# Norms, index scores and key choice of the first block moved in between its input projections; modulation blocks paired anew, the last one formed on VectorE

## The chip, the cores and the metric

One core of a Trainium2 chip runs the whole program. The metric is device time in microseconds (us), the median of three executions. Engines: TensorE (PE, its weight loads PEld), VectorE (DVE), ScalarE (ACT), GpSimd (POOL), and SyncE (SP), whose queue issues the weight loads.

## What is computed

Two transformer-like blocks on 256 tokens of width 1024, float32. The change lies in the first:

```python
ada = c @ w_ada + b_ada                      # 6 x 1024: shift1, scale1, gate1, shift2, scale2, gate2
h = rms_norm(x, g_norm1) * (1 + scale1) + shift1
z = h @ w_in                                 # 3524 wide: q 512, k 64, v 64, iq 256, ik 64, iw 4, p 512, gates 2048
q, k, ik = rms_norm(zq heads), rms_norm(zk), rms_norm(zik)
# index scores: for each query, sum over 4 heads of relu(iq . ik) * iw; the best 64 keys are attended
y_attn = dsa_attention(q, k, zv, iq, ik, iw) @ w_up_attn
y_pool = pool_mixer(zp, w_pool_grp, s_pool) @ w_up_pool    # means over windows 2, 4, 8, 16, then mixed per group
g_attn, g_pool = sigmoid(zg)
x = x + gate1 * ((g_attn * y_attn + g_pool * y_pool) @ w_out)
h2 = rms_norm(x, g_norm2) * (1 + scale2) + shift2
x = x + gate2 * peer_ffn(h2, ...)            # product-key experts: scores of 8 heads, top 16 of 16384 rows of u and v
```

The second block (recurrent branch, sparse attention, convolved feed-forward) isn't touched.

## The kernel before

All weights come through one stream of blocks, each 4 quarters of 512 KB. `plan()` writes out their order; two blocks that `PAIRED` joins are interleaved quarter by quarter (`quarter_no`). SP loads quarter b into `ring[b % 4]` once the quarter before it in that slot has left (L438), strictly in order. The blocks of `SPLIT` (in, pq, u, v and later ones) are split into a rounded part `high` (ScalarE, `round_quarter`, L925) and a rest `low` (POOL, L1918), four slots each, chosen by b % 4 too. `high` of a slot is written again only when TensorE has multiplied the quarter before in it; the ring slot is free when POOL is done. Split products are three matmuls (L340 to L342). up_pool, up_attn and out blocks are multiplied straight from the ring in float32 (L338; two matmul records for each product). `ahead(name, q)` on ScalarE rounds every split quarter up to three places beyond the named one, in ScalarE's own order of work.

The modulation (`ada0` to `ada11`, 512 columns each) is formed on VectorE as a running sum over the ring's quarters (L1453, L1455: 8 instructions a block) and then summed over the partitions by TensorE with a vector of ones (L475, or L470 and L471 for the two gate1 blocks 4 and 5). ada8 alone was multiplied on TensorE: 64 products of one column (L486).

Order in the first block: ada0 to ada3; the norm n1; in0 to in6 (`token_major`, 48 matmuls each), whose results ScalarE copies to Z (L1033). After the last one: VectorE's squares of q, k and ik (L1496, L1497), their norms into N1 (L1498 to L1517) and ScalarE's root; TensorE's pool means (L626) and pool mixing (L632) with ScalarE's copies (L1039, L1043) between; up_pool in three pieces, and between them the turning of N1 (L461) and the index products (L647). ScalarE applies relu to these (L1051), VectorE weights them into scores (L1527, L1529) and chooses keys by eight rounds of MAX8 and MATCH_REPLACE8 for each half of the tokens (L1540, L1541; the mask by L1543). ScalarE makes the sigmoids of the gates (L1054) and copies y_pool (L1059). TensorE sums ada6 and ada7, multiplies ada8, and starts the attention `a1`. Then up_attn; the mixture M1 on VectorE (L1558, L1559); its turning (L461 again); out0 and out1, gate1; the norm n2; the peer query pq0 and pq1 (eight quarters of 24 matmuls), and the peer stage: u and v.

Of the kernel before, what the change touches and what calls it, by code (L numbers as in the profile page):

```python
# [20 lines left out]
ACT = mybir.ActivationFunctionType  # L21
# [5 lines left out]
P = 128  # L27
S = 256
# [55 lines left out]
PAIRED = {"in2": "ada6", "in4": "ada7", "up_attn": "ada9", "out0": "ada4", "out1": "ada5", "pq0": "ada10",  # L84
# [43 lines left out]
def build_program(nc, a, out):  # L128
    ctx = ExitStack()
    with ctx:  # L130
# [78 lines left out]
        bias1 = hTl[:, 0:T, :]  # L209
# [245 lines left out]
        def _(pe):  # L455
# [23 lines left out]
            def ada_products(j):  # L479

                for q in range(QUARTERS):
                    wait_loaded(pe, f"ada{j}", q)
                    w = slot(f"ada{j}", q)
                    for k in range(4):
                        for c in range(2):
                            last = pe.matmul(PS[:, 7, 4 * j + k:4 * j + k + 1], w[:, c, k * P:(k + 1) * P],  # L486
                                             col("cT", 2 * q + c), start=(q == k == c == 0),
                                             stop=(q == QUARTERS - 1 and c == 1), skip_group_check=True)
                    free_slot(f"ada{j}", q, last)

# [126 lines left out]
            for i in range(Z1B):  # L617
# [4 lines left out]
            pe.wait_ge(sem("later_loaded"), LATER_ALL)  # L622
            pe.wait_ge(sem("z_kept"), 2 * Z1B)
            for g in range(4):
                for t in range(T):
                    last = pe.matmul(PS[:, 2 + g // 2, (g % 2) * S:(g % 2 + 1) * S],  # L626
                                     Z[:, t, P1 + g * P:P1 + (g + 1) * P], band[:, t, g, :],
                                     start=(t == 0), stop=(t == T - 1))
            last.then_inc(sem("pool_meaned"), 1)
            pe.wait_ge(sem("pool_means_kept"), 1)  # L630
            for g in range(4):
                last = pe.matmul(PS[:, 4 + g // 2, (g % 2) * S:(g % 2 + 1) * S], wpool[:, g, :], mixT[:, g, :],  # L632
                                 start=True, stop=True)
            last.then_inc(sem("pool_mixed"), 1)

            def up_pool(*quarters):
                token_major("up_pool", poolT, lambda t, o: 4 + 2 * t + o, per=1, inner=D, quarters=quarters)

            pe.wait_ge(sem("pool_kept"), 4)
            up_pool(0, 1)  # L640
            transposes("qk1", N1, "qk1_normed", 1)
            up_pool(2)
# [266 lines left out]
        def _(act):  # L909
# [120 lines left out]
            for i in range(Z1B):  # L1030
# [7 lines left out]
            act.wait_ge(sem("pool_meaned"), 1)  # L1038
            act.activation(mixT.rearrange("p g s -> p (g s)"), PS[:, 2:4, :].rearrange("p b n -> p (b n)"),  # L1039
                           ACT.Copy).then_inc(sem("pool_means_kept"), 1)  # L1040
            act.wait_ge(sem("pool_mixed"), 1)
            for g in range(4):
                act.activation(poolT[:, g, :], PS[:, 4 + g // 2, (g % 2) * S:(g % 2 + 1) * S], ACT.Copy,  # L1043
                               scale=col("spool", g)).then_inc(sem("pool_kept"), 1)
            keep_turned("qk1", NT1, lambda c: col("gain1", c))
            for t in range(T):
                n = (t + 1) * P
                act.wait_ge(sem("index_products"), t + 1)
                for e in range(2):
                    src = PS[:, 2 * t + e, :].rearrange("p (a s) -> p a s", a=2)[:, :, 0:n]  # L1050
                    act.activation(src, src, ACT.Relu).then_inc(sem("index_relu"), 1)  # L1051
            act.wait_ge(sem("z_kept"), 2 * Z1B)
# [4 lines left out]
            for t in range(T):  # L1057
                for half in range(2):
                    act.activation(y_pool[:, t, half * NB:(half + 1) * NB], PS[:, 4 + 2 * t + half, :],  # L1059
                                   ACT.Copy).then_inc(sem("y_pool_kept"), 1)  # L1060
            wait_used(act, "ada8")
            act.wait_ge(sem("ada_summed"), 6)
# [7 lines left out]
            for i in range(2):  # L1070
                act.wait_ge(sem("ada_summed"), 8 + i)
                act.activation(gate1[:, i * NB:(i + 1) * NB], PS[:, i, :],
                               ACT.Copy).then_inc(sem("gate1_kept"), 1)
# [245 lines left out]
        def _(dve):  # L1319
# [172 lines left out]
            ada(7)  # L1492

            dve.wait_ge(sem("z_kept"), 2 * Z1B)
            for t in range(T):
                link(dve.tensor_tensor(sq1[:, t, 0:576], Z[:, t, 0:576], Z[:, t, 0:576], ALU.mult))  # L1496
                link(dve.tensor_tensor(sq1[:, t, 576:640], Z[:, t, IK1:IK1 + HD], Z[:, t, IK1:IK1 + HD], ALU.mult))  # L1497
# [47 lines left out]
            dve.wait_ge(sem("chosen"), T)  # L1545
            attention("a1")
# [5 lines left out]
            ada(9)  # L1552
            wait_used(dve, "up_attn")
# [12 lines left out]
            dve.wait_ge(sem("ada_summed"), 7)  # L1566
# [5 lines left out]
            ada(4)  # L1572
            ada(5)
            dve.wait_ge(sem("gate1_kept"), 2)
# [12 lines left out]
            ada(10)  # L1587
            ada(11)
            for t in range(T):
                dve.wait_ge(sem("scores_kept"), 4 * (t + 1))  # L1590
                if t:
                    dve.wait_ge(sem("ada_summed"), ADA_B - 1)
                    dve.tensor_tensor(adaT[:, 40:48], PS[:, 7, 40:48], bada[:, 40:48],
                                      ALU.add).then_inc(sem("ada_kept"), 1)
# [484 lines left out]
```

## Time and profile before

| what | us |
|---|---|
| median of three executions (lowest, highest) | 1753.41 (1751.58, 1758.19) |
| the profiled execution; its span | 1753.76; 1752.0 |
| in0 to in6 on TensorE | 54.3 to 139.7 |
| attention a1 | 188.8 to 210.9 |
| end of pq1 | 321.4 |

The stretches of the profile count from the span's start. A stretch shows how long each engine was busy in it, the granted clock of TensorE as a share of full speed, and the DMA's share. In a list in order of time, the bracket holds the idle time of that engine ahead of the instruction and who ended it. Lines are those of the kernel before; a helper's line stands for all its calls. PS is PSUM, `region` a large SBUF area that holds most named tiles.

### The profile page before, as it was taken

How to read it: one execution, taken by the hardware profiler on the slowest of the kernel's cores; microseconds unless marked ns; L12 is line 12 of the kernel's file. 1: busy time of each engine (PE TensorE's matmuls, PEld its weight loads, DVE VectorE, ACT ScalarE, POOL GpSimd, SP SyncE). 2: the span in 40 equal slices, each digit the busy share in tenths (PEclk: the TensorE clock that was granted, in tenths of full speed). 3: DMA queues.
4: the chain of work that ended last, by engine and by line, in shares of the span. 5: the costliest groups of instructions: out<-in, count | busy, mean ns of one | idle time of the engine just before them, and what ended most of it. 6: DMA issues, size and time to landing. Idle time of an engine off the chain costs nothing. (4 is left out here: it accounts for less than half of the span.)

```text
span 1752.0 us, 27820 instructions
## 1 busy us (share of the span) xinstructions
PE 1615.5 (92%) x10015; PEld 1411.0 (81%) x10015; DVE 1162.1 (66%) x1691; ACT 866.8 (49%) x1471; POOL 1152.4 (66%) x468
## 2 busy tenths in 40 slices
PE   1898987899999999999999999999979988899999
PEld 1675635899999999988888888799857866789987
DVE  6334546799947777768888888661996276258760
ACT  1343203555557666645544445549744545354443
POOL 0680002688986666658888888658985730768887
PEclk9899687999999999989999999999989999999999
DMA  7572154555454444435555555446543620445554
GB/s 262 201 252 81 69 201 160 196 176 184 161 185 145 145 137 141 143 122 192 192 192 193 194 193 195 155 159 209 173 147 121 204 85 1 144 153 184 181 182 143
DMA packets 79272, 286.96 MB, mean 164 GB/s; under 512 B 8785, under 2 KB 9297, under 8 KB 79058
## 3 DMA queue, kind: packets, MB, share of 16 engines
q1 hardware_dynamic: 78464, 283.51, 48.4%
q10 hardware_dynamic: 722, 2.27, 0.4%
q8 instruction: 58, 0.95, 0.2%
q14 instruction: 28, 0.23, 0.0%
HBM read 284.70 MB, written 1.05 MB: 163 GB/s over the span
## 5 line engine op out<-in xcount | busy, mean ns | idle before, releaser
L1918 POOL TENSOR_TENSOR low<-ring,high 128x1024 fp32r<-128x1024 f32 x464 | 1152.2, 2495 | 589.0 <-ACT high L925 588.8
L925 ACT ACTIVATE high<-ring 128x1024 fp32r<-128x1024 f32 x464 | 488.7, 1058 | 439.1 <-PE PS L342 385.2
L340 PE MATMUL PS<-hTh,high 128*128 128x256 f32 (+1 forms) x1728 | 494.7, 286 | 11.3 <-POOL low L1918 10.2
L341 PE MATMUL PS<-hTl,high 128*128 128x256 f32 (+1 forms) x1728 | 490.0, 284 | 0.0
L342 PE MATMUL PS<-hTh,low 128*128 128x256 f32 (+1 forms) x1728 | 489.8, 283 | 0.0
L340 PE MATMUL PS<-high,hTh 128*128 128x512 f32 x960 | 379.9, 396 | 19.4 <-POOL low L1918 14.6
L341 PE MATMUL PS<-low,hTh 128*128 128x512 f32 x960 | 376.9, 393 | 0.0
L342 PE MATMUL PS<-high,hTl 128*128 128x512 f32 x960 | 376.4, 392 | 0.0
L340 PEld LDWEIGHTS PS<-hTh,high 128*128 128x128 f32 (+1 forms) x1728 | 323.9, 187 | 14.0 <-POOL low L1918 10.3
L1688 DVE TENSOR_TENSOR hTl<-region,hTh 128x256 fp32r<-128x256 f32 x128 | 289.1, 2260 | 60.4 <-ACT hTh L1141 60.4
L341 PEld LDWEIGHTS PS<-hTl,high 128*128 128x128 f32 (+1 forms) x1728 | 323.6, 187 | 0.1
L342 PEld LDWEIGHTS PS<-hTh,low 128*128 128x128 f32 (+1 forms) x1728 | 323.6, 187 | 0.0
L340 PEld LDWEIGHTS PS<-high,hTh 128*128 128x128 f32 x960 | 182.2, 190 | 63.9 <-POOL low L1918 15.8
L342 PEld LDWEIGHTS PS<-high,hTl 128*128 128x128 f32 x960 | 182.1, 190 | 38.6
L341 PEld LDWEIGHTS PS<-low,hTh 128*128 128x128 f32 x960 | 182.4, 190 | 37.1
L1114 ACT ACTIVATE onehot<-gate,gate_rest 128x128 fp32r<-128x128 f32 x256 | 82.0, 391 | 66.4 <-DVE gate L1650 66.4
L1455 DVE SCALAR_TENSOR_TENSOR region<-ring,cols,region 128x512 f32<-128x512 f32 x77 | 78.9, 1025 | 41.5 <-DMA ring<-in_stream 38.4
L1661 DVE TENSOR_TENSOR region<-region,PS 128x256 f32<-128x256 f32 (+31 forms) x64 | 35.2, 551 | 61.2 <-PE PS L730 61.2
L461 PE MATMUL PS<-ident,region 128*128 128x128 f32 x176 | 32.4, 361 | 39.1 <-ACT region L951 14.3
L338 PE MATMUL PS<-ring,region 128*128 128x512 f32 x128 | 62.9, 647 | 3.6 <-ACT region L1043 1.7
L461 PEld LDWEIGHTS PS<-ident,region 128*128 128x128 f32 x176 | 29.3, 192 | 43.5 <-ACT region L951 16.3
L730 PE MATMUL PS<-onehot 128*128 128x128 f32 x256 | 60.7, 276 | 0.0
(286 smaller groups left out, 1654.3 us busy)
## 6 DMA issues: line engine op xcount, KB each, us to landing
ring<-in_stream SPq DMA_DIRECT2D x536, 512.0 KB, 3.3
X<-in_x SPq DMA_DIRECT2D x1, 1024.0 KB, 5.1
region<-in_band ACTq DMA_DIRECT2D x1, 1024.0 KB
result<-X SPq DMA_DIRECT2D x4, 256.0 KB, 2.0
region<-in_skeys ACTq DMA_DIRECT2D x1, 512.0 KB
region<-in_consts ACTq DMA_DIRECT2D x1, 352.0 KB, 3.7
region<-in_wpool ACTq DMA_DIRECT2D x1, 256.0 KB
cols<-in_cols SPq DMA_DIRECT2D x1, 228.0 KB, 5.1
```

Of the source, the lines that this page charges most:

```text
L338: return pe.matmul(out_, stat, mov, start=start, stop=stop, **kw)
L340: pe.matmul(out_, sh, mh, start=start, stop=False, **kw)
L341: pe.matmul(out_, sh, ml, start=False, stop=False, **kw)
L342: return pe.matmul(out_, sl, mh, start=False, stop=stop, **kw)
L461: last = pe.transpose(PS[:, c // 2, (c % 2) * S + t * P:(c % 2) * S + (t + 1) * P], src[:, t, c * P:(c + 1) * P], ident[:, :])
L730: last = pe.matmul(dst, rows[:, j, :], rest[:, j, :], start=False, stop=True)
L925: act.activation(high[:, b % RING, :], ring[:, b % RING, :], ACT.Copy).then_inc(rounded[b % RING], 1)
L1114: ins = act.activation(fours(onehot[:, 2, g % 2, :])[:, j, :], fours(second[:, g % 2, :])[:, j, :], ACT.Copy, scale=gate_rest[:, 4 * g + j ...
L1455: ins = dve.scalar_tensor_tensor(ada_acc(j), w[:, c, :], col("cT", 2 * q + c), ada_acc(j), ALU.mult, ALU.add)
L1661: dve.tensor_tensor(v[:, 0:n, :], v[:, 0:n, :], placed[:, 0:n, :], ALU.mult)
L1688: dve.tensor_tensor(lo, src, hi.bitcast(F32), ALU.subtract).then_inc(sem("weights_split"), 1)
L1918: pool.tensor_tensor(low[:, b % RING, :], ring[:, b % RING, :], high[:, b % RING, :].bitcast(F32), ALU.subtract).then_inc(left[b % RING], 1)
```

## The change

The pairs of the stream change. Before: in2+ada6, in4+ada7, then up_pool, ada8 alone, up_attn+ada9, out0+ada4, out1+ada5, pq0+ada10, pq1+ada11. After: in1+ada6, in6+ada7, up_pool+ada8, up_attn+ada9, ada4 alone, out0+ada5, out1+ada10, pq0 alone, pq1+ada11. The number of quarters is the same. VectorE forms ada8 after ada7, both behind the key choice, and `ada_products` is gone. TensorE runs in0 to in2, the turning of N1, in3, the index products, in4, the pool means, in5, the pool mixing, in6, up_pool in one piece, the sums of ada6 to ada8, the attention. ScalarE makes the squares, and its root, relus and copies stand between the projections' copies, with calls of `ahead` in between. The mask `bias1` lies in `onehot` now, and the pool mixing and up_pool use other banks of PSUM. VectorE forms ada4 right after ada9 and ahead of the mixture, ada10 ahead of gate1's use. The diff, without changed counts of semaphores:

```diff
-PAIRED = {"in2": "ada6", "in4": "ada7", "up_attn": "ada9", "out0": "ada4", "out1": "ada5", "pq0": "ada10",
+PAIRED = {"in1": "ada6", "in6": "ada7", "up_pool": "ada8", "up_attn": "ada9", "out0": "ada5", "out1": "ada10",
           "pq1": "ada11"}
...
-    for name in [f"in{i}" for i in range(Z1B)] + ["up_pool", "ada8", "up_attn", "out0", "out1", "pq0", "pq1"]:
+    for name in [f"in{i}" for i in range(Z1B)] + ["up_pool", "up_attn", "ada4", "out0", "out1", "pq0", "pq1"]:
...
-        bias1 = hTl[:, 0:T, :]
+        bias1 = onehot[:, 0, :, 0:S]
...
 # TensorE
-            def ada_products(j):
...
+            for i in range(3):
+                z1(i)
+            transposes("qk1", N1, "qk1_normed", 1)
+            z1(3)
+            pe.wait_ge(sem("turned_kept"), kept_by("qk1", KC))
+            for t in range(T):
...
+                last.then_inc(sem("index_products"), 1)
+            z1(4)
             pe.wait_ge(sem("later_loaded"), LATER_ALL)
-            pe.wait_ge(sem("z_kept"), 2 * Z1B)
+            pe.wait_ge(sem("scored"), T)
             for g in range(4):
...
             last.then_inc(sem("pool_meaned"), 1)
+            z1(5)
             pe.wait_ge(sem("pool_means_kept"), 1)
...
             last.then_inc(sem("pool_mixed"), 1)
+            z1(6)
             pe.wait_ge(sem("pool_kept"), 4)
-            up_pool(0, 1)
-            transposes("qk1", N1, "qk1_normed", 1)
-            up_pool(2)
...
-            up_pool(3)
+            pe.wait_ge(sem("z_kept"), 2 * Z1B)
+            token_major("up_pool", poolT, lambda t, o: 4 + (2 + 2 * t + o) % 4, per=1, inner=D)
             pe.wait_ge(sem("y_pool_kept"), 4)
-            ada(6)
-            ada(7)
-            ada_products(8)
-            pe.wait_ge(sem("scored"), T)
+            for j in (6, 7, 8):
+                wait_used(pe, f"ada{j}")
+                ada(j)
             attention("a1")
...
 # ScalarE
+            z1(0)
+            z1(1)
+            act.wait_ge(sem("z_kept"), 4)
+            for t in range(T):
+                act.activation(sq1[:, t, 0:576], Z[:, t, 0:576], ACT.Square).then_inc(sem("sq1"), 1)
+                act.activation(sq1[:, t, 576:640], Z[:, t, IK1:IK1 + HD], ACT.Square).then_inc(sem("sq1"), 1)
+            ahead("in2", 1)
             act.wait_ge(sem("qk1_meansq"), 2)
             act.activation(st1[:, 1, :], st1[:, 0, :], ACT.Sqrt).then_inc(sem("qk1_root"), 1)
+            z1(2)
+            ahead("in3", 0)
             keep_turned("qk1", NT1, lambda c: col("gain1", c))
+            z1(3)
+            ahead("in4", 0)
             for t in range(T):
...
                     act.activation(src, src, ACT.Relu).then_inc(sem("index_relu"), 1)
+            z1(4)
+            ahead("in5", 1)
+            act.wait_ge(sem("pool_meaned"), 1)
...
+            z1(5)
+            ahead("in6", 0)
+            act.wait_ge(sem("pool_mixed"), 1)
...
+            z1(6)
...
 # VectorE
             ada(6)
-            ada(7)
-
-            dve.wait_ge(sem("z_kept"), 2 * Z1B)
-            for t in range(T):
-                link(dve.tensor_tensor(sq1[:, t, 0:576], Z[:, t, 0:576], Z[:, t, 0:576], ALU.mult))
-                link(dve.tensor_tensor(sq1[:, t, 576:640], Z[:, t, IK1:IK1 + HD], Z[:, t, IK1:IK1 + HD], ALU.mult))
+
+            dve.wait_ge(sem("sq1"), 2 * T)
             link(dve.tensor_reduce(st1[:, 2, :], sq1.rearrange("p t (h d) -> p (t h) d", d=HD), AX_X, ALU.add))
...
             dve.wait_ge(sem("chosen"), T)
+            ada(7)
+            ada(8)
             attention("a1")
...
             ada(9)
+            ada(4)
             wait_used(dve, "up_attn")
...
-            ada(4)
             ada(5)
+            ada(10)
             dve.wait_ge(sem("gate1_kept"), 2)
...
-            ada(10)
             ada(11)
```

## Rows read from the trace of the kernel before

**Rows 1.** the page: busy time by engine; a costly group (busy us, mean ns)
```profile
PE 1615.5 (92%) x10015; PEld 1411.0 (81%) x10015; DVE 1162.1 (66%) x1691; ACT 866.8 (49%) x1471; POOL 1152.4 (66%) x468
...
L925 ACT ACTIVATE high<-ring 128x1024 fp32r<-128x1024 f32 x464 | 488.7, 1058 | 439.1 <-PE PS L342 385.2
```

**Rows 2.** stretches: length, busy PE, PEld, DVE, ACT, POOL, PE clock, DMA share, GB/s
```profile
189.00:211.00 22.00, 20.88 (x120) 13.19 (x120) 12.74 (x33) 11.16 (x44) 0.00 (x0) 0.66 0.07 25
...
330.00:420.00 90.00, 90.00 (x740) 90.00 (x739) 82.81 (x335) 49.05 (x53) 75.23 (x32) 0.98 0.53 175
```

**Rows 3.** TensorE in order of time: start, length us, instruction [idle before it <-releaser]
```profile
145.99 2.00 PE L632 MATMUL PS<-region 128*128 128x256 f32 x8 [1.28 <-ACT region L1039]
...
149.65 7.13 PE L338 MATMUL PS<-ring,region 128*128 128x512 f32 x16 [1.66 <-ACT region L1043]
...
156.62 1.91 PE L461 MATMUL PS<-ident,region 128*128 128x128 f32 x16
...
171.61 3.57 PE L475 MATMUL PS<-ones,region 128*128 128x1 f32 x16 [4.51 <-ACT region L1059]
...
175.05 13.79 PE L486 MATMUL PS<-cols,ring 128*128 128x1 f32 x64
...
225.88 0.95 PE L475 MATMUL PS<-ones,region 128*128 128x1 f32 x8
...
232.07 3.68 PE L461 MATMUL PS<-ident,region 128*128 128x128 f32 x16 [5.24 <-DVE region L1560]
...
266.90 1.12 PE L470 MATMUL PS<-region,ones 128*128 128x512 f32 x2 [0.70 <-DVE region L1455]
```

**Rows 4.** VectorE in order of time, the norms and the key choice
```profile
143.00 1.49 DVE L1498 TENSOR_REDUCE region<-region 128x20 f32<-128x1280 f32 x1
...
148.56 0.07 DVE L1517 MEMSET region<- 128x8 f32 x1
...
166.75 0.11 DVE L1537 MEMSET region<- 64x64 f32 x1
...
180.82 0.29 DVE L1543 TENSOR_SCALAR hTl<-region 128x256 fp32r<-128x256 f32 x1
```

**Rows 5.** the projection in order of time; TensorE's waits (us, times, longest)
```profile
60.47 0.39 PE L342 MATMUL PS<-high,hTl 128*128 128x512 f32 x1
...
92.79 0.47 PE L340 MATMUL PS<-high,hTh 128*128 128x512 f32 x1 [1.32 <-POOL low L1918]
...
102.99 2.42 POOL L1918 TENSOR_TENSOR low<-ring,high 128x1024 fp32r<-128x1024 f32 x1 [0.91 <-ACT high L925]
...
PE PS L340 <- POOL low L1918: 11.7, 5, 7.8
```

**Rows 6.** VectorE and POOL together; one line's durations (ns min/median/max)
```profile
1329.56 10.88 DVE L1776 COPY region<-region 128x256 f32<-128x256 f32 x8
...
1330.24 7.33 POOL L1918 TENSOR_TENSOR low<-ring,high 128x1024 fp32r<-128x1024 f32 x3 [2.71 <-ACT high L925]
...
L1740 DVE TENSOR_TENSOR_SCAN region<-region x16: 658/2822/2836, 1226.7 to 1285.8; 84x256 f32<-84x256 f32 x16
```

**Rows 7.** MAX8 beside POOL by source line; ScalarE in order of time
```profile
L1609 DVE MAX8 region<-region x32: 428/428/430, 387.2 to 429.3; 128x8 f32<-128x256 f32 x32
...
169.52 2.04 ACT L1059 ACTIVATE region<-PS 128x512 f32<-128x512 f32 x4
```

**Rows 8.** TensorE and VectorE in order of time, up_attn and the mixture
```profile
211.63 14.41 PE L338 MATMUL PS<-ring,region 128*128 128x512 f32 x32 [0.69 <-ACT region L1067]
...
219.93 1.54 DVE L1455 SCALAR_TENSOR_TENSOR region<-ring,cols,region 128x512 f32<-128x512 f32 x2 [4.45 <-DMA ring<-in_stream]
...
226.08 0.70 DVE L1558 TENSOR_TENSOR PS<-PS,region 128x512 f32<-128x512 f32 x1 [0.93 <-PE PS L338]
```

**Rows 9.** the peer query: its stretch, and TensorE's waits
```profile
285.50:321.50 36.00, 28.18 (x192) 26.57 (x192) 28.66 (x23) 12.19 (x15) 18.38 (x8) 0.90 0.61 202
...
PE PS L340 <- POOL low L1918: 6.8, 5, 2.6
```

More of the change, by code:

```diff
@@ L477, in ada @@
                 last.then_inc(sem("ada_summed"), 1)
-            def ada_products(j):
[L481 to L489, printed above, removed]
             def wait_quarter(name, q):
@@ L616, in _, with z1 @@
             transposes("n1", XN1, "norm_scaled", nth_norm("n1", T, T))
-            for i in range(Z1B):
+            def z1(i):
                 if i >= 2:
@@ L620, in _ @@
                 token_major(f"in{i}", hT, lambda t, o, i=i: 4 + (2 * i + t) % 4, norm="n1" if i == 0 else None)
-            pe.wait_ge(sem("later_loaded"), LATER_ALL)
-            pe.wait_ge(sem("z_kept"), 2 * Z1B)
-            for g in range(4):
-                for t in range(T):
[L626 to L639, printed above, removed]
-            up_pool(0, 1)
+            for i in range(3):
+                z1(i)
             transposes("qk1", N1, "qk1_normed", 1)
-            up_pool(2)
+            z1(3)
             pe.wait_ge(sem("turned_kept"), kept_by("qk1", KC))
@@ L650, in _ @@
                 last.then_inc(sem("index_products"), 1)
-            up_pool(3)
+            z1(4)
+            pe.wait_ge(sem("later_loaded"), LATER_ALL)
+            pe.wait_ge(sem("scored"), T)
+            for g in range(4):
+                for t in range(T):
+                    last = pe.matmul(PS[:, 2 + g // 2, (g % 2) * S:(g % 2 + 1) * S],
+                                     Z[:, t, P1 + g * P:P1 + (g + 1) * P], band[:, t, g, :],
+                                     start=(t == 0), stop=(t == T - 1))
+            last.then_inc(sem("pool_meaned"), 1)
+            z1(5)
+            pe.wait_ge(sem("pool_means_kept"), 1)
+            for g in range(4):
+                last = pe.matmul(PS[:, g // 2, (g % 2) * S:(g % 2 + 1) * S], wpool[:, g, :], mixT[:, g, :],
+                                 start=True, stop=True)
+            last.then_inc(sem("pool_mixed"), 1)
+            z1(6)
+            pe.wait_ge(sem("pool_kept"), 4)
+            pe.wait_ge(sem("z_kept"), 2 * Z1B)
+            token_major("up_pool", poolT, lambda t, o: 4 + (2 + 2 * t + o) % 4, per=1, inner=D)
             pe.wait_ge(sem("y_pool_kept"), 4)
-            ada(6)
-            ada(7)
-            ada_products(8)
-            pe.wait_ge(sem("scored"), T)
+            for j in (6, 7, 8):
+                wait_used(pe, f"ada{j}")
+                ada(j)
             attention("a1")
@@ L1029, in _, with z1 @@
             split_high("n1")
-            for i in range(Z1B):
+            def z1(i):
                 wait_product(f"in{i}")
@@ L1051, in _ @@
                     act.activation(src, src, ACT.Relu).then_inc(sem("index_relu"), 1)
+            z1(4)
+            ahead("in5", 1)
+            act.wait_ge(sem("pool_meaned"), 1)
+            act.activation(mixT.rearrange("p g s -> p (g s)"), PS[:, 2:4, :].rearrange("p b n -> p (b n)"),
+                           ACT.Copy).then_inc(sem("pool_means_kept"), 1)
+            z1(5)
+            ahead("in6", 0)
+            act.wait_ge(sem("pool_mixed"), 1)
+            for g in range(4):
+                act.activation(poolT[:, g, :], PS[:, g // 2, (g % 2) * S:(g % 2 + 1) * S], ACT.Copy,
+                               scale=col("spool", g)).then_inc(sem("pool_kept"), 1)
+            z1(6)
             act.wait_ge(sem("z_kept"), 2 * Z1B)
@@ L1058, in _ @@
                 for half in range(2):
-                    act.activation(y_pool[:, t, half * NB:(half + 1) * NB], PS[:, 4 + 2 * t + half, :],
+                    act.activation(y_pool[:, t, half * NB:(half + 1) * NB], PS[:, 4 + (2 + 2 * t + half) % 4, :],
                                    ACT.Copy).then_inc(sem("y_pool_kept"), 1)
-            wait_used(act, "ada8")
-            act.wait_ge(sem("ada_summed"), 6)
+            act.wait_ge(sem("ada_summed"), 7)
             act.activation(adaT[:, 24:36], PS[:, 7, 24:36], ACT.Copy).then_inc(sem("ada_copied"), 1)
@@ L1070, in _ @@
             for i in range(2):
-                act.wait_ge(sem("ada_summed"), 8 + i)
+                act.wait_ge(sem("ada_summed"), 9 + i)
                 act.activation(gate1[:, i * NB:(i + 1) * NB], PS[:, i, :],
@@ L1591, in _ @@
                 if t:
-                    dve.wait_ge(sem("ada_summed"), ADA_B - 1)
+                    dve.wait_ge(sem("ada_summed"), ADA_B)
                     dve.tensor_tensor(adaT[:, 40:48], PS[:, 7, 40:48], bada[:, 40:48],
```

10 lines of the change are left out of this document (1 added, 9 removed).

## The prediction

> **What bounds the kernel now.** I read the page first [rows 1]: TensorE is busy in 92% of a 1752.0 us span, so what shortens the time must shorten TensorE's line of work. Then the stretches [rows 2]: the change touches 54 to 322 us, and from 330 on TensorE is busy 90.00 of 90.00 us, so all later work slides by what TensorE gains or loses up to there. Third, TensorE in order of time [rows 3]: the pool mixing with waits around it, up_pool in parts, the turning of N1, then a wait of 4.51 us, the sums of ada6 and ada7, and 13.79 us for the 64 thin products of ada8. The key choice on VectorE ends at 181.1 [rows 4], under these products, so the attention waits for TensorE, not for the choice. Last, the other engines where the change puts its work [rows 4 to 9].
>
> The profiled execution took 1753.76 us, 1.8 more than its span and 0.35 above the median of 1753.41. The sum is made on 1753.76 and 0.35 taken off.
>
> **Part 1, work off TensorE's line.** The products of ada8 go: 13.79. VectorE forms ada8 instead, and TensorE sums it in 8 thin products. 16 took 3.57 on a low clock, 8 took 0.95 on a full one [rows 3]: three blocks take 2.9 to 5.4; with the first of them on the full clock, 4.6, +1.0 over the 3.57. The waits of 1.28 and 1.66 us around the pool mixing are hidden, since ScalarE's copies now run under in5 and in6: -2.9. Before the sums TensorE waited 4.51 us because the sigmoids stood before the y_pool copies (2.04 [rows 7]). up_pool is now one piece of 14.4 us (32 matmuls, as up_attn [rows 8]) over the sigmoids, so only the copies and a handoff are left, 2.2: -2.3. The pool products, the turning, the index products and the mixing are moved, not saved. Together -18.0.
>
> **Part 2, the ring in the projection.** SP issues quarters in order into four ring slots. A paired projection uses only slots 0 and 2 of high and low, so a quarter can't be rounded before the one two ahead of it is multiplied. Of the 11.7 us that TensorE waited for POOL in the projection, 7.8 lay before in0 and 3.9 at in2 and in4, 1.32 of them ahead of in3, which so began at 92.79 after in2's end at 91.5 [rows 5]. With ada6 at in1, counted on from before's times: in1's quarter 0 is multiplied at 71.1, and quarter 2 then needs 1.06 of ScalarE [rows 1] and 2.4 of POOL [rows 5], 74.6, against 73.8: 0.8. in2's first quarter waits for the slot freed at 74.6, four us of DMA and 3.5 of splitting: 82.1 against in1's end at 80.1, 2.0. The squares, moved from VectorE to ScalarE (two of 128x576, two of 128x64, 1.7 us, by 0.51 for a copy of 128x512 [rows 7]), stand before in2's third quarter: 0.3 more. in2 ends near 93.4, +2.0. Pairing in6 costs one such wait, 0.8, where in4 had half of the 3.9 or a little less: -0.8. Bounds of both together: -1 and +4.
>
> **Part 3, the norms beside POOL.** The largest cost. With POOL idle they took from 143.0 to 148.6 [rows 4]: a reduce 1.49, two small scalings, a root on ScalarE, a reciprocal, and for each half one product, four scalings and a copy. Now they run from 84.5 on, while POOL splits quarters. Where the trace has both [rows 6], VectorE hardly advances while POOL runs: of the 10.88 us of eight copies, three POOL instructions in a row filled 7.33. Scans issued without waits between them took 2.82 against 0.66 at best, so a row of unlinked instructions isn't let through either. One VectorE instruction passes per POOL instruction when POOL has no gap.
>
> POOL's stock: in2's quarters 2 and 3 and all four of in3 can be split before the turning of N1, as high and low hold four. By 2.4 us each from 85.5, with one delay on ScalarE, the last ends near 100.5. Until then six to eight of the 14 exposed instructions have passed; some 1.5 us are left, and N1 is ready near 102.0. TensorE reaches the turning at 93.4 and waits 8.6. Bounds: nothing exposed (84.5 + 5.6 = 90.1, no wait), and all of the halves' work left (3.4 after 101.5, 11.5). I take 8.6, as [rows 6] lie at that end.
>
> An idle TensorE also loses its clock. After 5.24 idle us the 16 turns took 3.68, against 1.91 in a busy stretch [rows 3]; in0, begun at 54.3 after a long wait, had matmuls at full speed from 60.47 on [rows 5]. Six us at half rate cost 3.0; bounds 0 (short wait) and 4.7. Part 3: +11.6, bounds 0 and 16.
>
> The Trainium skill, "SBUF — State Buffer" (the port rules on VectorE and GpSimd), gives the same verdict: the shared pair is locked for a whole instruction, and tensor_reduce stays outside. By it the reduce keeps its 1.49; were it held too, this sum would be up to 2.4 higher.
>
> The choice is not held: MAX8 of 256 took 428 to 430 ns in all 32 cases of the peer stage [rows 7], where POOL was busy 75 of 90 us [rows 2]. From in3's end it needs 1.8 for index products and relu, 3.5 for scores, 14.3 for the choice [rows 4] and up to 4.8 for two exposed bias writes: 20 to 24. Behind it on VectorE stand ada7 and ada8, and behind ada7 the ring: its quarter 0, used 1 to 5 us later, frees the slot that SP waits for ahead of in6's last quarter. That quarter's own slot comes free 27.9 us after in3, and the split begins at 34.6, when in6's second quarter is multiplied. With 4 of DMA, VectorE is in time by 1 us at worst.
>
> To the attention: -18.0 + 2.0 - 0.8 + 11.6 = -5.2. The attention keeps its 22 us at clock 0.66 [rows 2]; were it at the full clock from the start, it would be some 4 shorter. Against this: a wait and thin sums stand ahead of it, as before.
>
> **Part 4, ada4 before the mixture.** VectorE now forms ada9 and then ada4 before it multiplies up_attn's result. ada4's third quarter takes the slot of up_attn's last one, freed at 226.04 when the matmuls end. A quarter of up_attn takes 3.60 (14.41 by four), so its first ended at 215.2; the two quarters that this let in were both readable 4.7 us later, at 219.93 [rows 8]. The last takes 1.54, so VectorE starts the mixture at 232.3 instead of 226.08. **+6.3**, and nothing hides it: M1, the turning of M1 and out0 wait behind it. Bounds 5 and 7.5. The clock is lost in either case.
>
> **Part 5, output and peer query.** ada5 comes with out0, so its sum no longer waits 0.70 for VectorE [rows 3]: -0.7. pq0 loses its partner, and two of its quarters are split before the norm. In 36.0 us TensorE was busy 28.18 for 192 matmuls [rows 9] that take 0.122 each further on (740 in 90 us [rows 2]), 23.4; five waits for POOL made 6.8, the rest was low clock. By POOL's 2.4 and the slots, pq0 runs through and ends near 299.7; pq1, still paired, waits once for 0.4: the end at 313.1 instead of 321.4, **-8**. Bounds -3 (one quarter's wait) and -9.
>
> Sum: -5.2 + 6.3 - 0.7 - 8.0 = -7.6, 1746.2, and against the median **1746**.
>
> **Rivals.**
> A, the norms hardly wait, as VectorE gets its instructions through in POOL's gaps. For it: a gap of 0.91 such as before 102.99 [rows 5] takes several scalings. Against it: [rows 6]. A wait of 1 and no lost clock give 1735.
> B, the peer query gives back only 3, since ScalarE or the DMA of two blocks sets the pace there: 1751. For it: DMA moved 202 GB/s there; against it: the waits named are for POOL [rows 9].
> C, slower: the choice is held by POOL as the norms are. Then some 11 of its 32 maxima and replacements pass before in6 starves; SP stands before ada7's third quarter, in6's last quarter comes 14 us late, and a clock lost after it costs 3: 1763. It decides from a choice that ends some 25 us after in3 on. Against it: the MAX8 row.
>
> **How the numbers follow.** The sum holds with 0.52 (its own range 1740 to 1751), A 0.18, B 0.16, C and other losses of its size 0.14. A measurement of this kernel tells about 0.5%, 8.8 us, from no change: the bounds are 1744.6 and 1762.2. Faster: A, and 0.22 of the sum's: 0.40. Slower: C, 0.14. Same: the rest, 0.46. The range 1734 to 1754 takes in A and B and leaves out C.
>
> **What would show it.** The turning of N1 after in2 with some 8 us idle before it, released by VectorE, and 3.6 us long. The 64 thin products gone, the attention starting 5 us earlier than 188.8. The mixture's first product some 6 us after up_attn's end, behind a DMA wait. pq0 and pq1 in 28 us. The prediction is wrong if VectorE's norm instructions together take under 6 us, if TensorE waits in in6 for POOL by more than 2, or if the attention starts earlier than 180.

## The result, and the profile after

The changed kernel took 1741.01 us (median of 6 executions, 1731.98 to 1744.67) beside 1752.49 for the kernel before (6 executions, 1748.00 to 1758.19). The ratio is 0.9919 [0.9897, 0.9941]: 14 us faster, 10 to 18. The profiled execution took 1738.60, its span 1736.8, 15.2 less than before's 1752.0. A second profile of the same kernel has a span of 1735.4 and the same waits.

The first rows to read are VectorE's norms, which answer to [rows 4]. In order of time: start, length, instruction, and in the bracket the idle time ahead of it.

```profile
82.46 1.49 DVE L1499 TENSOR_REDUCE region<-region 128x20 f32<-128x1280 f32 x1 [5.26 <-ACT region L1031]
83.98 1.92 DVE L1501 TENSOR_SCALAR region<-region 128x16 f32<-128x16 f32 x1
85.82 0.16 DVE L1503 TENSOR_SCALAR region<-region 128x4 f32<-128x4 f32 x1
87.08 0.28 DVE L1506 RECIPROCAL region<-region 128x20 f32<-128x20 f32 x1 [1.10 <-ACT region L1034]
87.39 1.40 DVE L1509 TENSOR_TENSOR region<-region 128x512 f32<-128x512 f32 x1
88.71 2.39 DVE L1513 TENSOR_SCALAR region<-region 128x64 f32<-128x64 f32 x1
91.02 2.40 DVE L1515 TENSOR_SCALAR region<-region 128x64 f32<-128x64 f32 x1
93.35 2.39 DVE L1513 TENSOR_SCALAR region<-region 128x64 f32<-128x64 f32 x1
95.66 2.38 DVE L1515 TENSOR_SCALAR region<-region 128x64 f32<-128x64 f32 x1
97.95 0.28 DVE L1517 COPY region<-region 128x256 f32<-128x256 f32 x1
98.27 0.69 DVE L1509 TENSOR_TENSOR region<-region 128x512 f32<-128x512 f32 x1
98.87 0.25 DVE L1513 TENSOR_SCALAR region<-region 128x64 f32<-128x64 f32 x1
```

GpSimd in order of time beside them:

```profile
83.46 14.52 POOL L1921 TENSOR_TENSOR low<-ring,high 128x1024 fp32r<-128x1024 f32 x6 [0.20 <-ACT high L914]
```

Six splits stand back to back until 97.98. From the first product (L1509) on, one VectorE instruction ends in each: the four scalings of 128x64, small as they are, take 2.38 to 2.40 us each. At 97.95, when the row of splits is over, the same scaling takes 0.25. Not everything is held: the reduce at the top keeps its 1.49 of [rows 4], the reciprocal its 0.28 in the middle of a split, and the scaling of 128x4 (L1503) ends 0.08 behind the held one before it.

Now TensorE, which answers to [rows 3]:

```profile
73.88 0.50 PE L340 MATMUL PS<-high,hTh 128*128 128x512 f32 x1 [0.94 <-POOL low L1921]
81.04 0.47 PE L340 MATMUL PS<-high,hTh 128*128 128x512 f32 x1 [1.32 <-POOL low L1921]
...
127.26 3.61 PE L628 MATMUL PS<-region 128*128 128x256 f32 x16
141.60 1.89 PE L635 MATMUL PS<-region 128*128 128x256 f32 x8
...
150.42 0.50 PE L340 MATMUL PS<-high,hTh 128*128 128x512 f32 x1 [1.47 <-POOL low L1921]
157.48 14.34 PE L338 MATMUL PS<-ring,region 128*128 128x512 f32 x32 [1.22 <-issue]
173.97 3.81 PE L475 MATMUL PS<-ones,region 128*128 128x1 f32 x24 [2.15 <-ACT region L1065]
...
200.51 14.36 PE L338 MATMUL PS<-ring,region 128*128 128x512 f32 x32 [0.69 <-ACT region L1072]
...
227.43 3.31 PE L461 MATMUL PS<-ident,region 128*128 128x128 f32 x16 [11.78 <-DVE region L1564]
...
262.19 3.70 PE L338 MATMUL PS<-ring,region 128*128 128x512 f32 x8
```

The turning of N1 starts at 100.00 after 7.8 idle us. The pool means and the mixing stand between projections without a wait. The thin products are gone; the 24 sums start at 173.97 and the attention at 177.7 (before 188.8). up_attn starts 11.1 earlier than in [rows 8], but the turning of M1 only 4.6 earlier: 11.78 idle us ahead of it instead of the 5.24 of [rows 3]. The sums and the peer query then run nearly without waits. TensorE's waits of the whole run, the ones that matter here (us, times, longest):

```profile
PE PS L340 <- POOL low L1921: 18.7, 14, 7.4
...
PE PS L461 <- DVE region L1564: 11.8, 1, 11.8
...
PE PS L461 <- DVE region L1518: 7.8, 1, 7.8
...
PE PS L461 <- DVE region L1773: 1.6, 1, 1.6
```

Why M1 is late is seen on VectorE:

```profile
214.86 0.49 DVE L1458 TENSOR_SCALAR region<-ring,cols 128x512 f32<-128x512 f32 x1 [0.99 <-DMA ring<-in_stream]
215.38 2.40 DVE L1460 SCALAR_TENSOR_TENSOR region<-ring,cols,region 128x512 f32<-128x512 f32 x3
218.35 3.18 DVE L1460 SCALAR_TENSOR_TENSOR region<-ring,cols,region 128x512 f32<-128x512 f32 x4 [0.57 <-DMA ring<-in_stream]
221.45 0.69 DVE L1562 TENSOR_TENSOR PS<-PS,region 128x512 f32<-128x512 f32 x1
```

ada4 runs from 214.86 on, its second half behind a transfer (L1460), and the mixture (L1562) starts 20.94 us after up_attn's start, where before it was 14.45 [rows 8]: +6.5.

### The profile page after: what moved, and what is told of

It is laid out like the page before. It is cut to its first block, busy times and chain, and to the rows that moved or that the text cites. A ratio compares the mean times of both kernels' runs of the same rounds, so it can differ in the third digit from the quotient of the medians.

```text
span 1736.8 us, 27719 instructions
## 1 busy us (share of the span) xinstructions
PE 1597.0 (92%) x9959; PEld 1398.7 (81%) x9959; DVE 1170.0 (67%) x1695; ACT 867.8 (50%) x1475; POOL 1153.6 (66%) x468
## 4 chain that ended last, share of the span: by engine, by line
PE 77%; DVE 11%; POOL 4%; ACT 3%; issue 3%; DMA 2%; ACTq 0%; SPq 0%; POOLq 0%; DVEq 0%
PE PS L340 22%; PE PS L341 21%; PE PS L342 21%; POOL low L1921 4%; PE PS L338 3%; DVE region L1743 2%; DMA ring<-in_stream 2%; PE PS L719 2%; PE PS L461 1%; PE PS L718 1%; DVE region L1460 1%; PE PS L783 1%; PE PS L551 1%; ACT region L979 1%; DVE region L1747 1%
## 5 line engine op out<-in xcount | busy, mean ns | idle before, releaser
L1460 DVE SCALAR_TENSOR_TENSOR region<-ring,cols,region 128x512 f32<-128x512 f32 x84 | 77.9, 927 | 55.4 <-DMA ring<-in_stream 52.1
L461 PE MATMUL PS<-ident,region 128*128 128x128 f32 x176 | 35.6, 387 | 54.3 <-ACT region L940 14.3
L338 PE MATMUL PS<-ring,region 128*128 128x512 f32 x128 | 57.4, 600 | 4.4 <-DVE region L1387 1.3
## 6 DMA issues: line engine op xcount, KB each, us to landing
cols<-in_cols SPq DMA_DIRECT2D x1, 228.0 KB, 5.0
```

What stands on the lines that cost most here:

```text
L338: return pe.matmul(out_, stat, mov, start=start, stop=stop, **kw)
L461: last = pe.transpose(PS[:, c // 2, (c % 2) * S + t * P:(c % 2) * S + (t + 1) * P], src[:, t, c * P:(c + 1) * P], ident[:, :])
L1460: ins = dve.scalar_tensor_tensor(ada_acc(j), w[:, c, :], col("cT", 2 * q + c), ada_acc(j), ALU.mult, ALU.add)
```

## Where the time came from

The two profiled executions, cut at places that both kernels have; times are differences of the points named.

| stretch | after minus before, us | forecast |
|---|---|---|
| start of in0 (before 54.34, after 53.48) | -0.9 | 0 |
| in0 to the end of in2 (before 37.14, after 38.71) | +1.6 | +2.0 |
| wait for N1 | +7.8 | +8.6 |
| turning of N1 on a low clock (3.33 to the next start, 1.75 before) | +1.6 | +3.0 with what follows it |
| in3 to in6 without what stands between (before 48.3, after 46.6) | -1.7 | -0.8 |
| the rest up to the attention | -19.5 | -18.0 |
| attention, up to up_attn | 0.0 | 0 |
| up_attn's start to the mixture | +6.5 | +6.3 |
| turning of M1 to the start of out1's last quarter (before 37.2, after 34.8) | -2.5 | -0.7 |
| that quarter (before 6.76, after 3.70) | -3.1 | 0 |
| the peer query (before 35.9, after 26.3) | -9.6 | -8.0 |
| peer query's end to the peer stage | +0.7 | 0 |
| **start of the peer stage** (before 329.2, after 310.2) | **-19.0** | **-7.6** |
| from there to the end | +3.8 | 0 |

These are two single executions, and the table holds for them. In the second profiles of the two kernels (experiments 9 and 10) the peer stage starts at 325.4 and 311.4, 14.0 apart instead of 19.0; and from there to the end the thirteen profiles of this study need 1417.0 to 1426.6 us, the kernel before alone 1422.8 and 1418.2, the changed one 1426.6 and 1424.0. So the last line is no larger than what one kernel's own executions differ by.

Still, one part of it has a pattern. From rgate's first product to the compressed logits of the second block the changed kernel needs 232.4 us in both of its profiles, the kernel before 228.0 and 227.6. TensorE of the changed kernel in that part, two turnings:

```profile
1307.58 1.94 PE L461 MATMUL PS<-ident,region 128*128 128x128 f32 x16 [1.56 <-DVE region L1773]
...
1323.19 3.25 PE L461 MATMUL PS<-ident,region 128*128 128x128 f32 x16 [2.77 <-DVE region L1784]
```

Before, the first of them ran at 1326.47 without a wait, and the other took 1.94, in both profiles. VectorE's eight products ahead of it, after and then (second fence) in the kernel before:

```profile
1295.78 11.53 DVE L1771 TENSOR_TENSOR region<-region 128x256 f32<-128x256 f32 x8
```

```profile
1315.67 9.43 DVE L1768 TENSOR_TENSOR region<-region 128x256 f32<-128x256 f32 x8
```

They take 2.1 us more, because they meet GpSimd's splits otherwise. GpSimd after, and then before:

```profile
1299.10 2.40 POOL L1921 TENSOR_TENSOR low<-ring,high 128x1024 fp32r<-128x1024 f32 x1 [1.56 <-ACT high L914]
```

```profile
1319.69 2.56 POOL L1918 TENSOR_TENSOR low<-ring,high 128x1024 fp32r<-128x1024 f32 x1 [2.28 <-ACT high L925]
```

The gap between two splits is 1.56 instead of 2.28, and TensorE is back at full clock earlier after an idle stretch of 10.6 us that both kernels have. The thirteen profiles fall into two groups without an overlap. In seven the second matmul behind the turning takes 0.39 to 0.59 us, the gap is 1.38 to 1.76, VectorE's eight products take 11.5 to 11.6, and TensorE has the wait, 1.45 to 1.72; in six the four figures are 0.63, 2.03 to 2.28, 9.4 to 9.6 and no wait. That fits a chain in which a faster TensorE frees a quarter earlier, so that GpSimd comes in earlier and holds VectorE longer; no experiment sets the clock there, so the order of cause stays argued. The change can't be said to cause it: the kernel before with ada8 alone moved has it, and the changed kernel's front half alone has it not.

## Experiments

**1 and 2: the two halves.** The changed kernel with the pairs from out0 on, and VectorE's ada4, ada5 and ada10, as before; and the kernel before with the new ones (VectorE's ada10 then stands ahead of gate1's use):

```diff
-PAIRED = {"in1": "ada6", "in6": "ada7", "up_pool": "ada8", "up_attn": "ada9", "out0": "ada5", "out1": "ada10",
+PAIRED = {"in1": "ada6", "in6": "ada7", "up_pool": "ada8", "up_attn": "ada9", "out0": "ada4", "out1": "ada5", "pq0": "ada10",
...
             ada(9)
-            ada(4)
             wait_used(dve, "up_attn")
```

```diff
-PAIRED = {"in2": "ada6", "in4": "ada7", "up_attn": "ada9", "out0": "ada4", "out1": "ada5", "pq0": "ada10",
+PAIRED = {"in2": "ada6", "in4": "ada7", "up_attn": "ada9", "out0": "ada5", "out1": "ada10",
...
             ada(9)
+            ada(4)
             wait_used(dve, "up_attn")
```

> The changed kernel up to the attention, but the pairs from the output projection on as before (out0+ada4, out1+ada5, pq0+ada10, pq1+ada11) and VectorE's blocks in the old places. If the two halves of the change are independent, the attention starts near 178 us, the mixture begins right at up_attn's end (the gap of 6.6 us falls to under 0.2), pq0 and pq1 take 36 us from the first matmul again instead of 26. If the last quarter of out1 was fast in the changed kernel (3.70 us for 8 matmul records against 6.76) because its sums no longer wait 0.7 us for VectorE, it is slow again here, 6.8. The peer stage then starts 3 to 7 us later than in the changed kernel (310.2): total 1744 to 1748. Rival: the clock of out1's last quarter is chance or comes from the longer idle stretch ahead of the turning of M1; then it can't be foretold from the 0.7 us. Second rival: the gain in the peer query comes from an earlier start and not from the pairs; then pq keeps its 26 us here and the total is near 1735.

> The kernel before up to the attention, with the new pairs from up_attn on (ada4 alone before out0, out0+ada5, out1+ada10, pq0 alone). Attention still at 188.8. If the halves are independent: the mixture begins 6.5 us after up_attn's end, out1's last quarter takes 3.7 us, pq0 and pq1 take 26: the peer stage starts 5 to 8 us earlier than before (329.2), at 321 to 324, total 1745 to 1748. Rival: ada4's wait cancels what the peer query gives, so that the peer stage starts within 2 us of 329.2.

Measured: the front half 1739.50 us (7 executions), ratio 0.9932 [0.9909, 0.9956]; the back half 1746.95 (12 executions), 0.9968 [0.9952, 0.9984]. By the ratios the front gives 12 us and the back 6, their sum 17.5 against 14 [10, 18] for the whole. In the front half's profile the attention starts at 176.2, the turning of M1 has its old 5.24 idle us, and the peer query lasts 35.6; in the back half's it lasts 26.3 from 287.2 on. The parts lie where the prediction put them, but the front gives more than twice the 5.2 forecast. The expectation for it, 1744 to 1748 with a peer stage 3 to 7 us later than in the changed kernel, failed: the front half alone is as fast as the whole change (1739.50 against 1741.01), so the 6 us that the back half gives by itself are not seen on top of it. The back half came out as expected, with the peer stage at 321.5.

**3: ada8 alone on VectorE.** In the kernel before:

```diff
 # TensorE
             ada(7)
-            ada_products(8)
+            wait_used(pe, "ada8")
+            ada(8)
...
 # VectorE
             dve.wait_ge(sem("chosen"), T)
+            ada(8)
             attention("a1")
```

> The kernel before, and only ada8 formed by VectorE after the key choice and summed in 8 thin products, in place of 64 thin products on TensorE (13.8 us). If the choice is the next thing to bind (it ends at 181.1, then 5.9 us for ada8's eight instructions and 1 to 1.8 for its sum), the attention starts at 188 to 189 as before, and the total moves by less than 1.5 us. Rival: what counts is TensorE's work; then the attention starts 12 us earlier and the total falls by 12.

Measured: 1750.58 us (10 executions), ratio 1.0001 [0.9978, 1.0024], no change. TensorE and, in the second fence, VectorE:

```profile
169.81 3.29 PE L475 MATMUL PS<-ones,region 128*128 128x1 f32 x16 [4.50 <-ACT region L1060]
185.62 1.87 PE L475 MATMUL PS<-ones,region 128*128 128x1 f32 x8 [12.53 <-DVE region L1455]
```

```profile
179.03 0.29 DVE L1543 TENSOR_SCALAR hTl<-region 128x256 fp32r<-128x256 f32 x1
179.35 0.49 DVE L1453 TENSOR_SCALAR region<-ring,cols 128x512 f32<-128x512 f32 x1
179.88 5.69 DVE L1455 SCALAR_TENSOR_TENSOR region<-ring,cols,region 128x512 f32<-128x512 f32 x7
```

The 13.79 us of thin products turn into 12.5 us of waiting: the choice ends at 179.3, and ada8 takes VectorE 6.2 more, so that the attention starts at 187.4 (before 188.8). The saving of 13.79 exists only because the choice moved into the projection. Both edits are one.

**4: four more scalings.** In the changed kernel, four scalings of 128x64 into a scratch area ahead of the norms' products, the values of N1 unchanged:

```diff
             link(dve.reciprocal(st1[:, 2, :], st1[:, 1, :]))
+            for i in range(4):
+                dve.tensor_scalar(work[:, 0, i * HD:(i + 1) * HD], Z[:, 0, K1:K1 + HD],
+                                  st1[:, 2, 8:9], None, ALU.mult)
```

> The changed kernel with four more scalings of 128x64 on VectorE, ahead of the first half's norms, into an unused tile. In the changed kernel one such instruction passes per POOL instruction (2.4 us each), until POOL has split all that high and low can hold (98 us). If POOL's stock is what ends the holding, TensorE's wait ahead of N1's turning grows only by the free time of what is pushed behind that point, from 7.8 to between 8.5 and 9.5 us. Rival, no such bound: each of the four costs a POOL instruction, and the wait grows by 9.6 to 17.4. Second rival, VectorE isn't held by POOL but is slow by itself in small instructions: all eight first ones take 2.4 us wherever they stand, also those behind 98 us.

Measured in one execution: 1738.92 us, a wait for N1 of 9.05, 1.2 more than in the changed kernel. VectorE:

```profile
88.56 8.12 DVE L1508 TENSOR_SCALAR region<-region 128x64 f32<-128x64 f32 x4
96.59 2.87 DVE L1512 TENSOR_TENSOR region<-region 128x512 f32<-128x512 f32 x1
99.39 0.24 DVE L1516 TENSOR_SCALAR region<-region 128x64 f32<-128x64 f32 x1
```

The four added ones are held in place of the kernel's own, which now run at 0.24. Four held instructions would have cost 9.6 more if each were charged; only 1.2 came. Of this the four free scalings make some 0.7; the rest is that in2 ended 0.5 us sooner after the reduce. What ends the hold is GpSimd's stock: `high` and `low` have four slots each and TensorE stands still. In the changed kernel GpSimd waits 9.90 us behind the sixth split for the next rounding, and ScalarE starts that at 106.74, released by TensorE's products of in3; here the row is six splits again, 14.05 us, with 11.55 of idle time behind it.

**5: the small work on ScalarE.** In the changed kernel the eight scalings and two copies of N1 go to ScalarE, ahead of its rounding; VectorE keeps the two products:

```diff
 # ScalarE, after the root
+            act.wait_ge(sem("qk1_inverse"), 1)
+            for t in range(T):
+                for dup in range(2):
+                    act.activation(N1[:, t, 512 + dup * HD:576 + dup * HD], Z[:, t, K1:K1 + HD], ACT.Copy,
+                                   scale=st1[:, 2, r0 + 8:r0 + 9])
...
```

> The changed kernel with the eight scalings of 128x64 and the two copies of 128x256 of the norms on ScalarE (which in the trace never waits for POOL's port); VectorE keeps the reduce, two small scalings, the reciprocal and the two products of 128x512. If POOL's hold on VectorE is the cause of the 7.8 us wait ahead of N1's turning, N1 is ready near 91 us, before in2's end at 92.2: the wait falls below 1 us, the turning takes 1.9 instead of 3.7 us, the attention starts near 168 instead of 177.7, and the total falls by 10 to about 1731. Rival: the wait comes from the length of the chain reduce, root, reciprocal, products, wherever its parts run; then it stays above 5 us. Second rival: ScalarE's two more microseconds delay the rounding of in3, and TensorE waits 2 to 4 us for POOL in in3 instead.

Measured: 1726.18 us (4 executions), ratio 0.9841 [0.9817, 0.9865]. TensorE, VectorE, ScalarE:

```profile
91.36 1.91 PE L461 MATMUL PS<-ident,region 128*128 128x128 f32 x16
```

```profile
86.67 4.38 DVE L1520 TENSOR_TENSOR region<-region 128x512 f32<-128x512 f32 x2
```

```profile
87.41 0.33 ACT L1041 ACTIVATE region<-region 128x64 f32<-128x64 f32 x1
87.64 0.40 ACT L1043 ACTIVATE region<-region 128x256 f32<-128x256 f32 x1
```

A scaling takes ScalarE 0.33 us beside the same row of splits. The two products are still held, 4.38 for 1.38 of work, but N1 is ready at 91.1, the wait is gone and the turning is at full clock, 1.91. The attention starts 10.6 earlier than in the changed kernel. The median is 14.8 lower, against 10 expected, and the profiled execution, the fastest of the four, gains only 8.2 of its 17.8 us up to the peer stage. So the 10.6 us are what is shown for N1; the rest of the median's gain is unexplained and no larger than the spread of the part behind the peer stage's start.

**6: ada4 ahead of up_attn.** In the changed kernel, both in the stream and on VectorE:

```diff
-    ... ["up_pool", "up_attn", "ada4", "out0", "out1", "pq0", "pq1"]:
+    ... ["up_pool", "ada4", "up_attn", "out0", "out1", "pq0", "pq1"]:
...
             ada(8)
+            ada(4)
             attention("a1")
...
             ada(9)
-            ada(4)
             wait_used(dve, "up_attn")
```

> The changed kernel with ada4's block ahead of up_attn in the stream and formed by VectorE before the attention. Its last quarters are let in when up_pool ends (171.8), readable near 176.5, summed by 178.0; VectorE's first instruction of the attention came at 179.2. If ada4's place is what kept the mixture waiting, the mixture starts within 0.2 us of up_attn's end instead of 6.6, the attention starts at most 0.5 later, and the peer stage starts 6 us earlier (304): total about 1735. Rival: the same wait for two quarters now stands ahead of the attention's first maximum, 3 us or more.

Measured: 1733.52 us (4 executions), ratio 0.9883 [0.9861, 0.9906]. TensorE:

```profile
208.87 7.13 PE L338 MATMUL PS<-ring,region 128*128 128x512 f32 x16 [0.16 <-DMA ring<-in_stream]
222.03 3.68 PE L461 MATMUL PS<-ident,region 128*128 128x128 f32 x16 [5.24 <-DVE region L1564]
```

The mixture starts at 216.04, right behind up_attn's end at 216.00, and the wait ahead of the turning of M1 is 5.24 again. The 6.5 us were ada4's place, not the mixture.

**7: both moves.** Experiments 5 and 6 together.

> Norm scalings on ScalarE and ada4 ahead of up_attn together. If the two waits are independent, the peer stage starts 16 us earlier than in the changed kernel, at 294, and the total is 1725 (0.984 of the kernel before). Rival: one uses up the other's gain, e.g. with the earlier in6 VectorE's ada7 and ada8 bind ahead of the attention; then no more than 10.

Measured: 1719.69 us (5 executions), ratio 0.9801 [0.9776, 0.9825], some 35 us under the kernel before and 21 under the changed one. The turning of N1 starts at 92.10 and takes 1.91, that of M1 at 212.13 behind 5.24 idle us, the peer stage at 295.2. This is the version to keep of the kernels here.

**8: the turning one projection later.** The other cure for the wait: in the changed kernel TensorE runs in3 ahead of the turning of N1, and all that follows moves one projection back, with ScalarE's work in the same order.

```diff
-            for i in range(3):
+            for i in range(4):
                 z1(i)
             transposes("qk1", N1, "qk1_normed", 1)
-            z1(3)
+            z1(4)
```

> The changed kernel with everything behind the norms one projection later: N1's turning after in3, index products after in4, pool means after in5, mixing after in6. The wait for N1 (7.8 us) and its cost in clock (2 us) go, since in3 covers it. But the key choice ends 20 us after in4, near 137, so VectorE uses ada7's first quarter near 139 and SP issues in6's last quarter only then: in6 waits about 6 us, and the mixing has exposed copies of 1.6. up_pool starts 2 to 4 us earlier than 157.5. Rival: the ring isn't held by the choice; then up_pool starts 8 us earlier.

Measured in one execution: 1739.96 us, span 1738.2. TensorE:

```profile
107.44 3.67 PE L461 MATMUL PS<-ident,region 128*128 128x128 f32 x16 [5.57 <-DVE region L1516]
...
156.25 0.79 PE L340 MATMUL PS<-high,hTh 128*128 128x512 f32 x1 [8.52 <-POOL low L1919]
```

I had expected the wait to be gone. It is 5.57: while TensorE multiplies in3 it frees slots, GpSimd splits in4's quarters into them, and VectorE's scalings are held (2.34 to 2.43 us each) until 106.6, where they were free from 98.9 on in the changed kernel. GpSimd's row is eleven splits here, from 79.67 to 106.66, and the hold ends with it, as it ended with six splits in the changed kernel. The choice then ends near 146 instead of 137.4, with ada7 behind it, and in6 starves: 8.52 us of waiting, where about 6 were expected; up_pool starts at 164.1 instead of 2 to 4 us earlier than 157.5. That is the chain of rival C, reached by a choice that starts later and not by one that is held.

**9 to 11: the profiles again.** The kernel before, the changed one and the front half, unchanged, one execution each, to see what varies from one execution to the next.

> The kernel before once more, for its profile alone. If the low clock in out1's last quarter (8 matmul records in 6.76 us, 3.70 at full clock) belongs to the 0.7 us that ada5's sum waits, it is there again. Rival: the fall of the clock in this stretch, and others later on, differ from execution to execution; then the quarter takes anything from 3.7 to 6.8 with the same 0.7 us wait.

> The changed kernel once more, for its profile alone. By the 0.7 us theory out1's last quarter takes 3.7 again, since its sums don't wait. By either theory the wait for N1 is again 7.5 to 8.5, the gap ahead of the mixture 6.0 to 7.0, the attention within 2 us of 177.7 less the shift of in0's start, and pq0 and pq1 26 to 27 us. If the clock varies by execution, later stretches show it at other places than in the first profile.

> The front half alone once more; its first profiled execution was the slowest of seven (1744.6, median 1739.5), with a wait of 1.9 us for ada5's sum and 6.7 us for out1's last quarter. By the 0.7 us theory both are there again. If they vary by execution, this one may show 3.7 and a peer stage 4 to 5 us earlier than 319.9.

Spans 1743.5, 1735.4 and 1732.5. The waits for N1 are 7.90 and 7.96 in the last two. The front half's peer stage begins at 309.6 here and at 319.9 in experiment 1, with the same code. Of these 10.3 us, 6.6 lie in ada5's sum, with its wait, and in the quarter behind it, and 2.4 in out0 and out1 ahead of them. The second profile of the kernel before, then the front half in experiment 1 and here:

```profile
262.65 1.12 PE L470 MATMUL PS<-region,ones 128*128 128x512 f32 x2 [1.01 <-DVE region L1455]
265.71 6.08 PE L338 MATMUL PS<-ring,region 128*128 128x512 f32 x8
```

```profile
256.28 2.08 PE L470 MATMUL PS<-region,ones 128*128 128x512 f32 x2 [1.89 <-DVE region L1460]
260.29 6.71 PE L338 MATMUL PS<-ring,region 128*128 128x512 f32 x8
```

```profile
251.46 1.13 PE L470 MATMUL PS<-region,ones 128*128 128x512 f32 x2 [0.20 <-DVE region L1460]
253.56 3.70 PE L338 MATMUL PS<-ring,region 128*128 128x512 f32 x8
```

A wait of 0.7 to 1.9 us ahead of ada5's sum goes with a last quarter of 6.1 to 6.8 us (three profiles), none or 0.2 with 3.70 (nine); the back half alone is the exception, with no wait and 5.39. Idle time as such doesn't decide it: with ada8 alone moved, TensorE waited 1.19 us for a transfer one quarter earlier, and both quarters behind it took 3.70.

## Why the prediction came out as it did

The forecast was 1746 in a range of 1734 to 1754; 1741.01 lies inside, on the faster side. In the ratio's terms, 14 us against the forecast 7.6 is nearly twice the gain. By the prediction's own bound of 1744.6 the median is "faster", to which it gave 0.40, and not "same", to which it gave 0.46. One of its three signs of being wrong came true: the attention starts at 177.7, earlier than 180, where the sum meant 183.6. The other two did not: the norms took from 82.5 to 99.9, and in6 waited 1.47 for POOL. So the time fell in the range although the stretch up to the attention was 5.9 us off and the one up to the peer stage 11.4; the 3.8 more that the part behind it took in this execution brought the total closer to the forecast, and that is luck. Rivals B (the peer query gives only 3) and C did not happen. Rival A's time of 1735 was closer to some executions than mine, but its mechanism was wrong: TensorE waited 7.8 us for the norms.

**Right, mechanism and nearly the size.** The hold of VectorE by GpSimd (7.82, 7.90 and 7.96 us measured, 8.6 forecast; experiments 4 and 5 show cause and bound). The choice not held: MAX8 of 128x256 took 0.43 us as in [rows 7], the two mask writes 1.65 and 1.01. ada4's place (+6.5 for +6.3; experiment 6 takes it back). The attention's 22 us. The peer query: 26.3 long, one wait of 1.23 where 0.4 was forecast, -9.6 for -8, a little beyond its bound of -9. By the Trainium skill ("SBUF — State Buffer", on who interferes with whom) tensor_reduce never contends with GpSimd on this chip; the 1.49 us beside a split agree.

**Too small, Part 1.** "Together -18.0" measured -19.5. The 24 sums took 3.81 where I had 4.6, and matmul groups set between projections overlap their neighbours: the index products took 1.58 in the list and the next start lay 1.51 behind theirs, the means 3.61 with 3.26, the mixing 1.89 with 1.55.

**Too small, Part 2.** "-0.8" for the pair moved from in4 to in6 measured -1.7. In the kernel before, the 1.32 ahead of in3 lay in this stretch and 1.63 more (the 11.7 of [rows 5] less 7.8, 1.32, and 0.95 inside in2), 2.95; after, 1.47 (the wait in in6). I had taken out only half of the 3.9 "or a little less" and left the 1.32 standing where my own cut put it.

**Too large, Part 3.** "Six us at half rate cost 3.0": the turning lost 1.6 and the start of in3 about 0.3, and the whole of Part 3 came to +9.7 for +11.6.

**The term that was most mis-sized, Part 5.** "-0.7" for the end of ada5's wait. It measured -2.5 and -3.1, in sum -5.5 and the largest miss: -3.1 in the quarter, -1.1 in the wait and the sums, and -1.4 in out0 and out1 ahead of them, which ada5 does not touch. In the second profiles of the two kernels the quarter gives -2.4 and the stretch ahead of it -1.5, none of it from out0 and out1 ahead of the sums (29.7 us before, 30.2 after), so those -1.4 are the spread of executions. [rows 3] has the wait of 0.70, and right behind the sums stands a quarter of eight matmuls that took 6.76, where the same eight take 3.6 at full clock; I read the wait and not the quarter behind it. The pairing of wait and slow quarter holds in twelve of the thirteen profiles, three of them with the wait; that the wait causes the low clock is argued from this pattern and not shown by an experiment that puts in a wait alone.

**What was not in it.** The +3.8 behind the peer stage. The late turnings above are in both profiles of the changed kernel and in neither of the kernel before, but single edits go either way, and the spread of this part is 9.6 us over all profiles. Whether any of it is a lasting cost of the changed kernel stays open. The misses of the early parts (-11.4) and of this one (+3.8) make 7.6 us of span. The rest, between the span's 15.2, the medians' 11.5 and the ratio's 14, is the spread of executions: the starts of in0 alone vary from 53.5 to 55.6 us.

## What to carry to other kernels

Before small VectorE instructions are placed beside a row of GpSimd instructions, count instructions and not elements: a product or a scaling of 128x64 costs up to one GpSimd instruction, until GpSimd runs out of buffers to fill. The reduce, the reciprocal and MAX8 were not held here. ScalarE did the same small work unheld. Work taken off TensorE is worth only what the engine that takes it has free ahead of its reader, so such a move is tried together with the one that frees that engine. In reading waits, read the matmuls behind a wait too: a wait of 0.7 us stood ahead of a quarter that took 3 us longer than at full clock.

## What the runs showed of the hardware

- The hold works instruction by instruction even for 128x64 scalings without waits between them: 2.38 to 2.40 us each beside splits of 2.4, 0.25 alone. GpSimd was little slowed there (14.52 for six); beside VectorE's products of 128x1024 at 1287 us two splits took 6.22.
- Beside the same splits a reciprocal of 128x20 kept its 0.28, MAX8 of 128x256 its 0.43 and MATCH_REPLACE8 of 128x256 its 0.41.
- TensorE after an idle stretch of 10.6 us returns to full speed at different moments: behind the same turning of 3.65 us, the second matmul took 0.41 in the changed kernel and 0.63 in the kernel before, and over thirteen profiles the earlier return went with a later wait of 1.45 to 1.72 us.
- Beside the same splits ScalarE took 0.33 us for a scaling of 128x64 and 0.40 for a copy of 128x256.
